# Heads of 64 dimensions as products over half the rows, and a changed order in five stages

## The reference

```python
def first_block(x, mem, ...):
    q_a, k_a, v_a, q_i, k_i, w_i, z_a, c_q, c_kv, k_rope, z_b, q_m, z_m, gate_logits = split(rms_norm(x) @ w_in)
    # A: 8 heads of 64; an index of 8 heads of 64 picks the 64 best keys of each query
    dots = einsum('bqhc,bsc->bhqs', q_i, k_i);  index = einsum('bhqs,bqh->bqs', relu(dots), w_i)
    o_a = softmax(q_a @ k_a.T over top_k(index)) @ v_a
    o_b = causal attention, 8 heads of 96, from the latents c_q and c_kv
    o_m = attention over mem, 4 heads of 128
    x = x + (sum of sigmoid(gate_n) * ((o_n * silu(z_n)) @ w_branch[n])) @ w_out

def second_block(x, mem, ...):
    # mixer: differential attention (DA, 4 heads, each a pair of 64) and gated linear attention (GLA, 4 heads of 64)
    p = probs(q1, k1) - lam * probs(q2, k2);  o = p @ v
    a_past = (q * e_pos) @ (k * e_neg).T;  a_fut = (q * e_neg) @ (k * e_pos).T
    a = where(lower, a_past, a_fut)
    h = h + concat(da, gla) @ w_o
    h = h + cross attention over mem, 4 heads of 256
    h = h + mixture of 32 experts, 2 a token (w_gate, w_up: 1024 x 512, w_down: 512 x 1024)
```

## Time and profile before

| | us |
|---|---|
| median of 3 runs | 1124.64 (1123.66 to 1125.01) |
| the profiled execution | 1124.0 |
| its span (first to last instruction) | 1122.2 |
| PE busy | 925.8 (83%) |
| PE's weight loads | 581.2 (52%) |
| DVE busy | 404.1 (36%) |
| POOL busy | 247.3 (22%) |
| ACT busy | 170.3 (15%) |
| bytes moved | 290.38 MB, mean 259 GB/s |

### The profile page before, as it was taken

One profiled execution on the slowest core, in us unless ns is written; L12 is line 12 of the kernel. 1 busy time (PEld: TensorE's weight loads), 2 busy tenths in 40 slices (PEclk: granted clock), 3 DMA queues, 4 the chain that ended last, 5 costly groups with the idle time before them and its releaser, 6 DMA issues.

```text
span 1122.2 us, 12455 instructions
## 1 busy us (share of the span) xinstructions
PE 925.8 (83%) x5006; PEld 581.2 (52%) x5006; DVE 404.1 (36%) x984; ACT 170.3 (15%) x370; POOL 247.3 (22%) x368
## 2 busy tenths in 40 slices
PE   6999999999999999989999999655656557473847
PEld 3775487789999878865544555221211213131312
DVE  5537935762223655866545424010000101010101
ACT  2114232431001003013312311000000000000000
POOL 4543141234753948930000000000000000000000
PEclk9999999999999999999999999887786978687889
DMA  7636242224445344524219458999999999999997
GB/s 281 195 121 225 80 145 76 76 76 150 154 170 208 109 152 155 203 93 150 79 71 350 180 225 371 425 429 428 428 428 428 426 428 428 428 428 428 429 421 276
DMA packets 64312, 290.38 MB, mean 259 GB/s; under 512 B 9015, under 2 KB 11902, under 8 KB 52222
## 3 DMA queue, kind: packets, MB, share of 16 engines
q1 hardware_dynamic: 58206, 205.16, 47.6%
q10 hardware_dynamic: 6048, 84.41, 17.7%
HBM read 288.51 MB, written 1.05 MB: 258 GB/s over the span
## 4 chain that ended last, share of the span: by engine, by line
PE 56%; DMA 29%; DVE 5%; POOL 5%; ACT 2%; issue 2%; SPq 1%; another core or an unknown queue 1%; DVEq 0%; ACTq 0%; POOLq 0%
PE ACC L530 11%; DMA ring<-in_w_e_down_dram 10%; DMA PJ<-in_w_e_down_dram 10%; PE ACC L545 8%; PE ACC L668 7%; PE ACC L671 7%; PE ACC L569 5%; DMA BIG<-in_w_e_gate_dram 4%; DMA ring<-in_w_e_gate_dram 4%; POOL ring L1298 4%; PE AUX L1097 4%; PE AUX L1061 3%; PE ACC L953 2%; PE AUX L580 2%; PE AUX L700 1%
## 5 line engine op out<-in xcount | busy, mean ns | idle before, releaser
L1298 POOL TENSOR_TENSOR ring<-ring 128x256 f32<-128x256 f32 x272 | 204.5, 782 | 173.7 <-PE ACC L668 72.4
L1061 PE MATMUL AUX<-ring,R 128*32 128x512 f32 x400 | 132.7, 716 | 41.8 <-DMA BIG<-in_w_e_up_dram 20.7
L545 PE MATMUL ACC<-BIG,ring 128*128 128x256 f32 (+1 forms) x464 | 106.2, 382 | 0.0
L545 PEld LDWEIGHTS ACC<-BIG,ring 128*128 128x128 f32 (+1 forms) x464 | 84.6, 187 | 15.6 <-issue 3.6
L2305 DVE SCALAR_TENSOR_TENSOR GB<-GB,AUX 128x512 f32<-128x512 f32 x8 | 5.5, 688 | 235.0 <-ACT GB L1683 235.0
L1061 PE MATMUL AUX<-R 128*32 128x512 f32 x176 | 60.7, 707 | 25.6 <-DMA ring<-in_w_e_up_dram 11.0
L1061 PE MATMUL AUX<-BIG,R 128*32 128x512 f32 x176 | 64.0, 737 | 20.3 <-DMA PJ<-in_w_e_up_dram 20.3
L1097 PE MATMUL AUX<-ring,BIG 128*32 128x512 f32 x160 | 60.2, 707 | 21.9 <-DMA R<-in_w_e_down_dram 12.3
L530 PE MATMUL ACC<-ring,BIG 128*128 128x512 f32 (+2 forms) x192 | 76.0, 554 | 0.0
L1061 PE MATMUL AUX<-SQE,R 128*32 128x512 f32 x112 | 61.6, 713 | 16.9 <-DMA ring<-in_w_e_up_dram 9.8
L1061 PEld LDWEIGHTS AUX<-ring,R 128*32 128x32 f32 x400 | 31.4, 129 | 76.0 <-issue 76.0
(11 more groups left out here) (345 smaller groups left out, 1422.3 us busy)
## 6 DMA issues: line engine op xcount, KB each, us to landing
ring<-in_w_in_dram SPq DMA_DIRECT2D x20, 2048.0 KB, 7.9
ring<-in_w_e_gate_dram SPq DMA_DIRECT2D x8, 2048.0 KB, 39.2
ring<-in_w_e_up_dram SPq DMA_DIRECT2D x6, 2048.0 KB, 41.9
ring<-in_w_e_gate_dram ACTq DMA_DIRECT2D x6, 2048.0 KB, 27.8
ring<-in_w_e_down_dram SPq DMA_DIRECT2D x5, 2048.0 KB, 40.1
ring<-in_w_e_up_dram ACTq DMA_DIRECT2D x5, 2048.0 KB, 24.2
ring<-in_w_ckv_dram SPq DMA_DIRECT2D x4, 2048.0 KB, 8.1
BIG<-in_w_e_down_dram SPq DMA_DIRECT2D x4, 2048.0 KB, 21.7
```

Source lines behind the costliest of these rows:

```text
L545: mm = nc.tensor.matmul(bank[0:m, j * S:(j + 1) * S], w[:, i, a + j * P:a + j * P + m], rhs[:, i, :], start=(i == 0), stop=(i == k - 1))
L1061: mm = nc.tensor.matmul(bank[r, :], M_xt[:, k, r], w[e][:, k, :], start=(k == 0), stop=(k == KD - 1))
L1298: ins = g.tensor_tensor(out[:, k, :], a[:, k, :], b[:, k, :], op)
```

## The change

- Index, A, DA: queries are drained as they are turned (`QT4`, `drain_turned`), and a head is multiplied over its own 64 rows, the two heads of a pair one after the other into different banks. `score_both` makes the scores of both query tiles of a pair of heads at once, in every second step; the four `AUX` banks are views of two tiles `PAIR`, so that DVE reads two banks in one instruction. `QPAD` and POOL's two clears of it go. Each pair of `dots` takes two banks, and ACT takes it in two pieces.
- `dots` go between the products of `ka`, one pair behind every second product.
- Attention A: steps 0 to 5 between the products of `zb`, the rest between those of `qm`; ACT's tanh and DVE's silu of `zb` behind step 5, DVE's `combine("qm")` in four parts between the last steps.
- GLA: products over 64 rows, alternating between the halves and two banks; POOL sums the weights of `gg` before its three decay products.
- First loads: gains and positions are issued by ACT; the first half of `mk`'s weights comes in two pieces with a semaphore each; PE turns the gains first, and `mk` waits for each quarter of mem only where it reads it.
- Cross attention: `xk` is drained behind the quarter (0, 1); the second `start_sum` is split around a score; ACT drains a turned tile before it makes the next exponentials.

```diff
@@ -200,7 +200,8 @@
         ACC = [ctx.enter_context(nc.psum_tensor(f"ACC{i}", [P, 1024], F32)) for i in range(2)]
-        AUX = [ctx.enter_context(nc.psum_tensor(f"AUX{i}", [P, 512], F32)) for i in range(4)]
+        PAIR = [ctx.enter_context(nc.psum_tensor(f"PAIR{i}", [P, 1024], F32)) for i in range(2)]
+        AUX = [PAIR[i // 2][:, i % 2 * 512:i % 2 * 512 + 512] for i in range(4)]
@@ -523,8 +522,13 @@
                     for i in range(k):
-                        if (name, t, i) == ("mk", 0, 4):
-                            wait_chunk(name)
+                        if name == "mk":
+                            if i % 4 == 0:
+                                wait_drained(pe, ("mem", t, i // 4))
+                            if t == 0 and i in (0, 2):
+                                pe.wait_ge(first_landed[i // 2], 16)
+                            elif (t, i) == (0, 4):
+                                wait_chunk(name)
@@ -592,13 +596,28 @@
+            def score_both(u, h):
+
+                full = [aux(SB0 + i, ("S", u + i))[1] for i in range(2)]
+                for t in range(TT):
+                    nk = keys_of(t)
+                    for i in range(2):
+                        r = slice(64 * i, 64 * i + 64)
+                        mm = nc.tensor.matmul(AUX[SB0 + i][:, t * P:t * P + nk], QT4[r, h, t * P:(t + 1) * P],
+                                              KT4[r, h, 0:nk], start=True, stop=True)
+                        if t == TT - 1:
+                            mm.then_inc(full[i], 1)
...
                 for s in range(a, U + 3 if b is None else b):
-                    if s < U:
+                    if s < U and name in ("A", "DA"):
+                        if s % TT == 0:
+                            score_both(first_unit[name] + s, units[name][s][1])
+                    elif s < U:
@@ -759,15 +773,16 @@
                 wait_drained(pe, ("ki", t))
-            for n in range(8):
+            def dots(n):
...
                 nk = keys_of(t)
-                bank, full = aux(n % 4, ("dots", n))
+                full = [aux(2 * (n % 2) + i, ("dots", n, i))[1] for i in range(2)]
                 for i in range(2):
-                    mm = nc.tensor.matmul(bank[:, i * nk:(i + 1) * nk], QPAD[:, 2 * h + i, t * P:(t + 1) * P],
-                                          KIT[:, 0:nk], start=True, stop=True)
-                mm.then_inc(full, 1)
-            project("ka", XT3)
+                    r = slice(64 * i, 64 * i + 64)
+                    nc.tensor.matmul(AUX[2 * (n % 2) + i][:, 0:nk], QT4[r, h, t * P:(t + 1) * P], KIT[r, 0:nk],
+                                     start=True, stop=True).then_inc(full[i], 1)
+
+            project("ka", XT3, after=lambda done, total: dots(done // 2 - 1) if done % 2 == 0 else None)
@@ -775,8 +790,9 @@
             tiles = [(name, t) for t in range(TT) for name in ("qa", "ka")]
-            project_t("zb", XT3, after=spread("A", 0, 11, begin=7, ready=tiles + ["va"]))
-            project_blocks("qm", XT3, T_x, x0_sums)
+            project_t("zb", XT3, after=spread("A", 0, 6, begin=7, ready=tiles + ["va"]))
+            project_blocks("qm", XT3, T_x, x0_sums,
+                           after=lambda done: attend("A", 5 + done // 5, 6 + done // 5) if done % 5 == 0 else None)
@@ -850,13 +866,15 @@
                 bank, full = acc(("intra", t))
-                for h in range(4):
-                    nc.tensor.matmul(bank[:, h * P:(h + 1) * P], KNZ[:, h, t * P:(t + 1) * P],
-                                     QP[:, h // 2, t * P:(t + 1) * P], start=True, stop=True)
-                for h in range(4):
-                    mm = nc.tensor.matmul(bank[:, 512 + h * P:512 + (h + 1) * P], KPZ[:, h, t * P:(t + 1) * P],
-                                          QN[:, h // 2, t * P:(t + 1) * P], start=True, stop=True)
-                mm.then_inc(full, 1)
+                for hh in range(2):
+                    for T3, q_, a in ((KNZ, QP, 0), (KPZ, QN, 256)):
+                        for i in range(2):
+                            r = slice(64 * i, 64 * i + 64)
+                            c = 512 * i + a + hh * P
+                            mm = nc.tensor.matmul(bank[:, c:c + P], T3[r, 2 * hh + i, t * P:(t + 1) * P],
+                                                  q_[r, hh, t * P:(t + 1) * P], start=True, stop=True)
+                            if (hh, a, i) == (1, 256, 1):
+                                mm.then_inc(full, 1)
@@ -937,11 +955,11 @@
-            def start_sum(t, last):
+            def start_sum(t, last, halves=range(2)):
...
                     wait_drained(pe, ("wo", t_))
-                for h in range(2):
+                for h in halves:
@@ -1005,10 +1023,11 @@
             attend("C", 0, 1)
+            start_sum(1 - first_sum, ("wcq", 1, 1), [0])
...
             turn(3, ("xq", 1, 1))
-            start_sum(1 - first_sum, ("wcq", 1, 1))
             attend("C", 1, 2)
+            start_sum(1 - first_sum, ("wcq", 1, 1), [1])
@@ -1148,10 +1167,6 @@
             sp.dma_start(R1v, rows(A["mem"])).then_inc(mem_landed, 16)
-            for dst, src in gains:
-                sp.dma_start(dst, src).then_inc(gains_landed, 16)
-            sp.dma_start(pos_i[:, :], A["positions"][0].rearrange("(t p) -> p t", p=P),
-                         allow_slow_non_contiguous=True).then_inc(pos_landed, 16)
@@ -1159,7 +1174,8 @@
                     if c == 0:
-                        sp.dma_start(dst[:, 0:4, :], src[:, 0:4, :]).then_inc(first_landed, 16)
+                        for i in range(2):
+                            sp.dma_start(dst[:, 2 * i:2 * i + 2, :], src[:, 2 * i:2 * i + 2, :]).then_inc(first_landed[i], 16)
@@ -1370,11 +1384,11 @@
                 weight_sums(name)
+            weight_sums("gg")
...
             g.tensor_tensor(KE, kt(GK, 2), kt(EE, 2), ALU.mult).then_inc(gla_products, 1)
-            weight_sums("gg")
@@ -1429,17 +1443,21 @@
-            def drain_padded(key, dst):
-
-                t = key[1]
-                view = dst.rearrange("p (h i) q -> p h i q", i=2)
-                drain(key, [(view[64 * i:64 * i + 64, :, i, t * P:(t + 1) * P],
-                             lambda b, i=i: b[64 * i:64 * i + 64, :].rearrange("p (k q) -> p k q", k=4)) for i in range(2)])
-
-            def soften(name, a=0, b=None):
+            def soften(name, a=0, b=None, drain_first=False):
+
+                def take_turned(s):
+                    u = first_unit[name] + s - 2
+                    nk = keys_of(units[name][s - 2][0])
+                    n = nk if name == "DA" else 2 * nk
+                    bank = wait_full(act, ("T", u))
+                    if u >= 2:
+                        wait_full(act, ("O", u - 2))
+                    a_.activation(buf(PT, u)[:, 0:n], bank[:, 0:n], ACT.Copy).then_inc(free_sem(("T", u)), 1)
...
                 for s in range(a, U + 2 if b is None else b):
+                    if s >= 2 and drain_first:
+                        take_turned(s)
@@ -1449,16 +1467,14 @@
                         last.then_inc(exped, 1)
-                    if s >= 2:
-                        u = first_unit[name] + s - 2
-                        nk = keys_of(units[name][s - 2][0])
-                        n = nk if name == "DA" else 2 * nk
-                        bank = wait_full(act, ("T", u))
-                        if u >= 2:
-                            wait_full(act, ("O", u - 2))
-                        a_.activation(buf(PT, u)[:, 0:n], bank[:, 0:n], ACT.Copy).then_inc(free_sem(("T", u)), 1)
...
-
+                    if s >= 2 and not drain_first:
+                        take_turned(s)
...
+
+            for dst, src in gains:
+                act.dma_start(dst, src).then_inc(gains_landed, 16)
+            act.dma_start(pos_i[:, :], A["positions"][0].rearrange("(t p) -> p t", p=P),
+                          allow_slow_non_contiguous=True).then_inc(pos_landed, 16)
@@ -1525,10 +1542,11 @@
             for t in range(TT):
-                drain_padded(("qa", t), QPAD)
+                drain_turned(("qa", t), QT4, 4)
                 drain_turned(("ka", t), KT4, 4)
-            soften("A")
+            soften("A", 0, 6)
             tanh_of("zb", ZT[:, 1024:2048])
+            soften("A", 6)
@@ -1637,15 +1655,16 @@
                     drain(key, [(CQN[:, t, h * 512:(h + 1) * 512], lambda b: b[:, 0:512])])
-                    if (t, h) == (1, 0):
+                    if (t, h) == (0, 1):
...
                                 drain_turned(("xk", k, g), CK8[:, 4 * g:4 * g + 4, :], 4)
+                    if (t, h) == (1, 0):
...
                 drain_turned(("xq", 1, g), CQ8[:, 4 * g:4 * g + 4, :], 4)
-            soften("C")
+            soften("C", drain_first=True)
@@ -1791,10 +1810,14 @@
                 bank = wait_full(dve, ("S", u))
+                b = bank[:, 0:2 * nk].rearrange("p (i k) -> p i k", i=2)
+                if name in ("A", "DA"):
+                    if t == 0:
```

(24 more changed lines are left out.)

39 lines of the change are left out of this document (18 added, 21 removed).

## The result

The changed kernel takes 1112.4 us (median of four, 1111.24 to 1112.81), the kernel before 1124.2 (1123.66 to 1125.01): ratio 0.9893, interval 0.9879 to 0.9906. That is 11.8 us less, where 19.8 were forecast. The profiled execution took 1112.29 us, its span is 1110.6.

The account below looks back on a forecast made before the run. DMA bytes bind the late part, started by PE's chain ahead of SP's load at 675.61 us. Terms 3.6 - 1.0 + 5.5 + 3.9 + 3.0 + 4.8 = 19.8 us off 1124.0, so 1104.8 us as median; range 1100 to 1114.

Parts of the forecast that it names:

- A: Rival: the 64-row halves do not run side by side; 9.3 us of the gain lost, 1114.1 us; chance 0.15.
- rival B: Only pairs of 128 columns gain nothing, if both halves' weight loads go in turn; 3.5 lost, 1108.3 us; chance 0.12.
- Rival C: New loops bring waits between mask and normalize that eat attention A's term; 5.5 us lost, 1110.3 us; chance 0.11.
- The thesis: From slice 24 on DMA bytes bind; one us less on PE ahead of SP's load at 675.61 is one less overall.
- The price of a visit: Going into and out of row halves on PE costs 0.15 us; a head's scores take 0.80 us instead of 1.30.
- 1. First loads: Start of the kernel: mk's products from about 9.5 us instead of 12.16, at full clock; 3.6 us gained (1.5 to 4.5).
- 2. Dots into ka: PE passes ka 2.3 us earlier but waits 2.6 for POOL's rope, with clock loss; -1.0 us (0 to -4).
- 3. Attention A: Attention spread over zb and qm, from turns to qm's end: 40.3 us instead of 45.5; term 5.5 us (2 to 8).
- 4. gg and intra: GLA: gg's sums ahead of decay products save 2.3 us, intra in halves 1.6; term 3.9 us (1 to 5).
- 5. DA: Attention DA: four heads save 2.0 us of PE work, DVE's wait for the second score 0.8; term 3.0 (0 to 3.5).
- 6. Cross: Cross attention: PE waits of 1.76 and 0.82 us go, 2.2 more ahead of wco; term 4.8 us (2.5 to 5.5).
- E: Rival: slower than before, score banks force a full round per head in attentions A and DA; 1130 us; chance 0.03.

Follow-up runs that it names:

- both maps on the upper rows: Changed kernel with both score products of a tile on the upper 64 rows in attentions A and DA, lower rows left out (one half only): 3115.02 us.
- the scores twice: Changed kernel with each head's scores in attentions A and DA computed twice into the same place inside one visit: 1116.59 us.
- attention A in zb: Changed kernel with attention A inside zb alone again, PE, ACT and DVE in the old order, row halves kept: 1113.62 us.
- the norm moved: Changed kernel with DVE's norm of qa and ka put between the second and third of its eight selection steps: 1108.57 us.
- the late parts alone: Kernel before with only gg's sums ahead of the decay products and the cross attention edits; no row halves, old first loads: 1116.84 us.
- the three repairs: Changed kernel with mem turned ahead of the gains, DVE's norm inside the selection, and dots of two heads per visit in ka: 1105.93 us.
- x ahead: Kernel with the three repairs, plus four gains on SP ahead of mk's weights and x ahead of their second half: 1105.79 us.

## Why the prediction was right and where it was not

**The number.** 1112.4 lies inside the range 1100 to 1114, and outside the 1101 to 1108 that the forecast gave itself. The range was wide enough because of rivals A, B and C, and none of these is what happened. So the thesis and the direction were foreseen, but that the range held the time is luck.

**The thesis** was right. In thirteen profiled kernels (the kernel before, the changed one and eleven others; the one with both maps on the upper rows aside) the span from SP's load to the end is 446.2 to 447.5 us, while the load moved between 656.2 and 675.6. (The prediction misreads one digit of the earlier trace rows: slice 24, counted from 0, is an 8, and the nines begin with 25. Nothing hangs on it.)

**The price of a visit** was the step that failed most widely. I took 0.15 us for going in and out, from the four column-split records of the earlier trace rows, and counted the neighbours as free. The changed kernel shows 0.42 us for two products of 128 columns, 0.63 of 256, 0.85 for a head and 1.99 for the 32 records of intra (485.19 to 487.18): always columns at double rate plus 0.20. Besides, four records of 512 columns between visits take 1.91 us for 1.72: 0.19 more. A visit costs 0.4. The same stood in the rows of before, one line lower than I looked: behind the value products four records of 256 columns take 0.96 us (165.88 to 166.84), beside plain products 0.87 (158.61 to 159.48). The Trainium skill ("TensorEngine Tiling (Array Packing)", Key Properties) says that a change of mode drains TensorE; the 0.4 us a visit fits that, though no row shows the drain itself, and I had priced it with less than half of what it costs.

**1. First loads** (3.6 forecast, -0.7 measured). Three things were wrong. Gains at 6.2: they landed at 9.11, behind weights issued beside them. x 1.8 us earlier: it landed at 14.9, 0.4 earlier, and was squared at 16.24 where it was at 15.40, because ACT first waits for mem's scale, which hangs on the gains. And the main one, shown by the run with the gains on SP: even with mk at 10.95 the gain is not passed on, because ACT's sine and DVE's angles stand ahead of the drain of mk's bank. I had put 0.6 on that, it takes all of it. The sine came 2.4 us later than before (35.49 for 33.08), of which 0.84 is x's start. The other 1.6 I overlooked: the way from x's squares over DVE to the sine took 19.25 us for 17.68, as more of DVE's work fell beside POOL's sums of weights. In the changed kernel:

```profile
31.41 0.18 DVE L1944 TENSOR_SCALAR PJ<-PJ 128x32 f32<-128x32 f32 x1
...
33.33 2.78 POOL L1313 TENSOR_TENSOR ring<-ring 128x256 f32<-128x256 f32 x4 [1.99 <-PE ACC L690]
...
34.81 0.65 DVE L1950 TENSOR_SCALAR PJ<-PJ 128x32 f32<-128x32 f32 x1
35.49 0.26 ACT L1483 ACTIVATE PJ<-PJ 128x64 f32<-128x64 f32 x1 [15.77 <-DVE PJ L1950]
```

DVE's operations on 2 or 32 columns take 0.16 to 0.19 us here while POOL is idle, and nearly all that overlap its sums take 0.6 to 0.7. With the gains on SP it was worse (19.46 us from x's squares to the sine): an earlier mk let POOL's last four sums follow without a pause. In all nine kernels in which PE waits in mv for ACT, cq starts 6.74 or 6.75 us behind the sine, wherever mk began. That POOL's work slows DVE's is read from these rows; no run moved it.

**2. Dots into ka** (-1.0, measured -3.4). The lateness of rope was foreseen: DVE's accumulation ended ten us later (126.59 for 116.61) and POOL's mark with it. That the wait was 2.14 us for 2.6 forecast is luck in part: rope came at 154.86 for 152.4, and PE at 152.72 for 149.8. What failed is "PE passes ka 2.3 us earlier". Taking the 55.0 us of the plain products off the stretch from qa's products to the turns (and the wait), the dots cost PE 6.1 us before, 6.0 in the changed kernel, 5.6 in a block and 4.2 in four visits: eight visits give back what the overlap gains. The clock took 1.35 here, and 0.4 more behind it in zb, where I had put 0.7.

**3. Attention A** (5.5, measured 4.8). Near, by two errors that cancel. From zb to the end of qm I had 35.6 us of work and 2.9 of waits; it became about 38.8 of work, 0.4 of that by the slow clock, and 0.5 of waits. Four visits for scores and eight for value products lie in it, and the 0.2 us that each costs its neighbours, 2.4 in all by this estimate, I had not counted; the loop I stepped through waits less than I thought. Rival C, that waits eat this term, was wrong.

**4. gg and intra** (3.9, measured 3.9). Right in both parts: 2.5 to KE's transposes, 1.6 for intra, less 0.2 on the transposes beside it. The 1.99 us there also settle rival B: 32 records of 128 columns in one visit do run at double rate, so weight loads don't hold short pairs. The rule of the Trainium skill ("TensorE: Matmul & The Clock Gate", LDWEIGHTS) that a load's time goes by its columns would have kept them at the old rate only if the halves' loads went one after the other.

**5. DA** (3.0, measured 2.2): PE's idle time fell from 2.7 to 1.9 us, the 0.8 of the forecast, though its waits for DVE grew (0.4 to 1.0) and those for ACT shrank. Its work fell by 1.4 for 2.0 priced; the four visits, 0.25 us dearer each, are more than that gap.

**6. Cross** (4.8, measured 4.1). The wait of 1.76 is gone (from wo's products to the transposes at 603.54 it is 1.9 us less than before). Ahead of wco 2.2 came where I had put 3.0: PE's waits there were 0.82, 0.58, 0.63 and 0.21 before, 2.2 in all, so I had priced more than there was to take, and 0.44 is left at 626.67.

**The rivals.** The measured time lies near that of A (halves not side by side, 1114.1; with intra at 3.7 for 1.95 its sum is 0.2 too low), but A is refuted by the run on one half and by intra. E did not come: no head shows a round trip. What came was no rival of mine: a dearer visit and a first stage tied to other engines.

## What to carry to other kernels

Products over 64 rows side by side pay per visit, here 0.4 us, so gather them: 32 records in one visit took 1.99 us for 3.57, eight visits of two products each gained nothing. When an operation is moved later on the bound engine, follow what hangs on its last piece through every engine: one reordered norm on DVE was worth 3.8 us, a third of the whole change, 1.7 of it by the clock that fell behind the wait. A load brought forward is worth only what the drains behind the first products let through; look for the next wait before pricing it, and for what runs beside the engine that it hangs on.

## What the hardware showed that was not expected

The clock after a wait. Behind a wait of 2.14 to 2.18 us the sixteen qa turns took 3.30, 2.96, 1.97, 1.97, 3.42, 2.58, 1.97 and 1.97 us in the eight kernels that have that wait. Where they were slow, zb's first products were too, and the two together lost the same in each: 1.7 us in four kernels (the changed one, the gains on SP, the scores twice, attention A in zb), nothing in the other four. The granted clock in the changed kernel, and with mem turned first:

```profile
156.40:157.96 1.56, 1.56 (x10) 1.56 (x8) 0.00 (x0) 1.19 (x2) 1.48 (x3) 0.50 1.05 410
```

```profile
153.94:155.74 1.80, 1.80 (x16) 1.80 (x17) 0.16 (x1) 1.11 (x3) 1.80 (x3) 1.00 1.04 387
```

Behind 2.23 to 2.27 us near 396 the rest of the stretch took 7.0 us in four kernels (before among them) and 5.8 in the ten others. So a wait of this length costs nothing or about 1.2 to 1.7 us, and no cause in the programs was found. Differences of one or two us in the end between these kernels are not to be read without it.

Slow products at a granted clock of 1.00. mk's first products last 0.85 us in the changed kernel too (the weight loads start at 13.68, 14.53, 15.37, then 15.80), half the rate of the later ones (0.43), yet the window says 1.00, where it said 0.52 before:

```profile
12.80:14.80 2.00, 2.00 (x5) 0.97 (x4) 1.67 (x8) 0.00 (x0) 0.00 (x0) 1.00 1.01 407
```

I had expected full speed there because PE would not have been idle before; with sixteen transposes ahead and no idle time between, it was still slow. But with the norm moved, where nothing of this stage is changed, mk's loads start at 12.50, 13.04 and 13.47, at full rate almost from the first product. So this too differs from execution to execution. From mk's start to x's transposes it took 13.7 to 16.2 us in the kernels here. Where PE waits in mv for ACT this decides nothing (with the norm moved the transposes came 1.5 us earlier than in the changed kernel, and cq 0.15 later); it counts in the four kernels without that wait whose own products set cq's start: before, the late parts alone, the three repairs, and x ahead.
